# Latent attention: query and key blocks as one paired product for the operand's two parts, emptied by two engines

## What is computed

```python
def _mla_mixer(x, cos, sin, w_in, q_norm, w_qb, kv_norm, w_kvb, w_out):
    proj = x @ w_in
    c_q, c_kv, k_rope, z = jnp.split(proj, [512, 1024, 1088], axis=-1)
    q = (_rmsnorm(c_q, q_norm) @ w_qb).reshape(b, s, 16, 192)
    q_nope, q_rope = q[..., :128], q[..., 128:]
    kv = (_rmsnorm(c_kv, kv_norm) @ w_kvb).reshape(b, s, 16, 128 + 128)
    k_nope, v = kv[..., :128], kv[..., 128:]
    q_rope, k_rope = _rope(q_rope, cos, sin), _rope(k_rope, cos, sin)
    attn = _chunk_causal_attention([q_nope, q_rope], [k_nope, k_rope], v)
    return (attn * jax.nn.silu(z)) @ w_out
```

## Time and profile before

| | us |
|---|---|
| median of 3 runs | 1971.5 (1971.48 to 1973.13) |
| the profiled execution | 1971.0 |
| its span, first to last instruction | 1969.5 |
| granted TensorE clock in the span | 1.00 (2.4 GHz) |

### The profile page before, as it was taken

How to read it: one execution, slowest core, us unless ns; L and a number is a source line. 1 busy time by engine, 2 the same in 40 slices (tenths; PEclk the granted TensorE clock), 3 DMA queues, 4 the chain that set the end, 5 groups by cost and what they waited for, 6 DMA issues and landing times.

```text
span 1969.5 us, 28727 instructions
## 1 busy us (share of the span) xinstructions
PE 1963.2 (100%) x11370; PEld 1716.8 (87%) x11370; DVE 1368.8 (69%) x2117; ACT 1049.3 (53%) x1640; POOL 0.2 (0%) x4
## 2 busy tenths in 40 slices
PE   9999999999999999999999999999999999999999
PEld 7889988988888888898888888888888888888888
DVE  6756778986567676898778887666665556666554
ACT  5645555765456754575566655544443344444432
POOL 0000000000000000000000000000000000000000
PEclk9999999999999999999999999999999999999999
DMA  8554325455543455545533345555555555555562
GB/s 323 184 184 168 129 107 193 171 198 193 192 143 136 180 186 190 192 172 195 214 129 145 118 163 193 192 191 193 192 186 181 192 190 192 193 185 186 190 213 103
DMA packets 52874, 353.43 MB, mean 179 GB/s; under 512 B 5781, under 2 KB 9373, under 8 KB 11013
## 3 DMA queue, kind: packets, MB, share of 16 engines
q1 hardware_dynamic: 50016, 348.84, 48.9%
q10 hardware_dynamic: 2724, 2.75, 0.4%
HBM read 349.47 MB, written 2.11 MB: 179 GB/s over the span
## 4 chain that ended last, share of the span: by engine, by line
PE 94%; DVE 4%; ACT 1%; issue 0%; DMA 0%; ACTq 0%; DVEq 0%
PE bank L1117 94%; DVE WL L2052 2%; DVE AR L2229 0%; ACT WH L1542 0%; DVE AR L2342 0%; DVE XP L2225 0%; DVE AR L2339 0%; DVE XP L2327 0%; PE bank L1256 0%; DMA X<-in_x 0%; DVE AR L2218 0%; DVE AR L2253 0%; DVE AR L2252 0%; ACT XP L1673 0%; ACT L1555 0%
## 5 line engine op out<-in xcount | busy, mean ns | idle before, releaser
L2052 DVE TENSOR_TENSOR WL<-raw,WH 128x1024 fp32r<-128x1024 f32 x649 | 787.7, 1222 | 311.7 <-ACT WH L1542 304.2
L1542 ACT ACTIVATE WH<-raw 128x1024 fp32r<-128x1024 f32 x649 | 681.9, 1056 | 452.6 <-PE bank L1117 421.0
L1117 PE MATMUL bank<-XP,WH 128*128 128x512 f32 (+2 forms) x2096 | 668.4, 393 | 1.0 <-DVE WL L2048 0.6
L1117 PEld LDWEIGHTS bank<-XP,WL 128*128 128x128 f32 x2016 | 378.8, 188 | 80.4 <-issue 0.7
L1117 PE MATMUL bank<-FP,WH 128*128 128x512 f32 x1408 | 443.3, 396 | 0.0
L1117 PE MATMUL bank<-XP,WL 128*128 128x256 f32 (+1 forms) x2016 | 409.8, 279 | 0.1
L1117 PEld LDWEIGHTS bank<-XP,WH 128*128 128x128 f32 (+1 forms) x2096 | 329.1, 188 | 8.0 <-DVE XP L2095 1.4
L1117 PEld LDWEIGHTS bank<-FP,WL 128*128 128x128 f32 x1408 | 265.0, 188 | 61.6
L1117 PE MATMUL bank<-FP,WL 128*128 128x256 f32 x1408 | 277.5, 278 | 0.0
L1117 PE MATMUL bank<-AP,WH 128*128 128x512 f32 x704 | 222.1, 396 | 0.0
L1117 PEld LDWEIGHTS bank<-FP,WH 128*128 128x128 f32 x1408 | 215.2, 189 | 0.4
(11 more groups left out here) (325 smaller groups left out, 1708.8 us busy)
## 6 DMA issues: line engine op xcount, KB each, us to landing
raw<-in_W SPq DMA_DIRECT2D x326, 1024.0 KB, 4.8
out<-AR ACTq DMA_DIRECT2D x16, 128.0 KB, 2.4
raw<-in_W SPq DMA_DIRECT2D x3, 512.0 KB, 6.6
X<-in_x SPq DMA_DIRECT2D x3, 512.0 KB, 12.5
AR<-rv SPq DMA_DIRECT2D x1, 1024.0 KB, 5.9
cst<-in_cst SPq DMA_DIRECT2D x1, 899.5 KB, 12.1
raw<-in_W SPq DMA_DIRECT2D x2, 256.0 KB, 4.1
AR<-in_sgu SPq DMA_DIRECT2D x1, 512.0 KB, 5.7
```

The costliest lines, as they stand in the source:

```text
L1117: return pe.matmul(o, lhsT, rhs, start=start, stop=stop)
L1542: ac.activation(w_slot(WH, s), raw_half(hf), ACT.Copy).then_inc(s_hi, 1)
L2052: tt(w_slot(WL, s), raw_half(pl.half_of[s]), w_slot(WH, s).bitcast(F32), ALU.subtract).then_inc(s_lo, 1)
```

## The change

The three kinds of stage become paired, with VectorE as the last to empty them. Each of their 160 tiles issues two products in place of three, each of the 40 blocks fills a whole bank, and each is emptied in two steps: ScalarE copies the second half to the destination, VectorE adds the first half to it. `head_part` names the destination for both engines. The banks, their turns, and the order of the list of steps are the same.

```diff
@@ -400,9 +400,9 @@
 
 STAGES = {}
 for _s in [Stage("c", 9, 16, "dve", 7, 0, (0, 1, 2, 3, 4, 5, 6)), Stage("z", 16, 16, "dve"),
-           *(Stage(f"qr{g}", 2, 4, "act", pair=False) for g in range(4)),
-           *(Stage(f"qn{g}", 4, 4, "act", pair=False) for g in range(4)),
-           *(Stage(f"kn{g}", 4, 4, "dve", pair=False) for g in range(4)), *(Stage(f"v{g}", 1, 4, "act", 0, 512) for g in range(4)),
+           *(Stage(f"qr{g}", 2, 4, "dve") for g in range(4)),
+           *(Stage(f"qn{g}", 4, 4, "dve") for g in range(4)),
+           *(Stage(f"kn{g}", 4, 4, "dve") for g in range(4)), *(Stage(f"v{g}", 1, 4, "act", 0, 512) for g in range(4)),
            Stage("wo0", 16, 16, "dve", 3, 0, (0, 1, 2), half=False, norm=0), Stage("conv", 16, 16, "dve", (AHEAD, 4), 0, (0, 1, 2, 4, 3, 5, 6, 7), ahead=AHEAD),
            Stage("gates", 1, 16, "dve", pair=False),
            Stage("vm", 4, 16, "act", 0, 512), Stage("o", 16, 16, "dve"), Stage("mz", 16, 16, "dve"),
@@ -880,6 +880,10 @@
         mx = [small[:, 8 * i:8 * i + 2] for i in range(2)]
         ss = [small[:, 16 + 8 * i:16 + 8 * i + 2] for i in range(2)]
         sc = float(192 ** -0.5)
+
+        def head_part(kind, g, n):
+
+            return qr[g % 2][n] if kind == "qr" else blk(QKN, 2 * (4 * g + n) + (kind == "kn"))
 
 
         LN_D = [ar(0, 4096), ar(8192, 4096)]
@@ -1613,13 +1617,10 @@
                 h = n
                 if what == "hi":
                     hi(n)
-                elif what[:2] in ("qr", "qn") and what[3:] == " out":
-                    name, g = what[:3], int(what[2])
-                    ac.wait_ge(*done(name, n))
-                    if what[:2] == "qr" and g >= 2:
-                        ac.wait_ge(s_rope, g - 1)
-                    to = qr[g % 2][n] if what[:2] == "qr" else blk(QKN, 2 * (4 * g + n))
-                    ac.activation(to, bank[pl.bank_of[name, n, 0]][:, 0:T], ACT.Copy).then_inc(s_out["act"], 1)
+                elif what[:2] in ("qr", "qn", "kn") and what[3:] == " out":
+                    if what[:2] == "qr" and int(what[2]) >= 2:
+                        ac.wait_ge(s_rope, int(what[2]) - 1)
+                    second_half(what[:3], n, head_part(what[:2], int(what[2]), n))
                 elif what[0] == "v" and what[2:] == " out":
                     g = int(what[1])
                     ac.wait_ge(*done(what[:2], 0))
@@ -2176,10 +2177,8 @@
                         ins = tt(B[q1, :], x1[q2, :], rt[0][q2, :], ALU.subtract)
                     ins.then_inc(s_rope, 1)
                     dv.wait_ge(s_rope, n + 1)
-                elif what[:2] == "kn" and what[3:] == " out":
-                    name, g = what[:3], int(what[2])
-                    dv.wait_ge(*done(name, n))
-                    dv.tensor_copy(blk(QKN, 2 * (4 * g + n) + 1), psum(name, n)).then_inc(s_out["dve"], 1)
+                elif what[:2] in ("qr", "qn", "kn") and what[3:] == " out":
+                    whole(what[:3], n, head_part(what[:2], int(what[2]), n))
                 elif what == "max":
                     S, m = bank[3 + h % 2], mx[h % 2]
                     dv.wait_ge(s_msc, h + 1)
```

## The result

| | before | after |
|---|---|---|
| median of 12 runs, us | 1971.97 (1971.15 to 1973.13) | 1976.45 (1976.16 to 1976.84) |
| ratio | | 1.0022, 95% interval 1.0014 to 1.0030 |
| profiled execution, us | 1971.0 | 1976.5 |
| span, us | 1969.5 | 1975.0 |
| granted TensorE clock | 1.00 | 1.00 |

The account below looks back on a forecast made before the run. TensorE's uninterrupted products were taken to bound the kernel. Waits and restarts of 6.8 us less 1.9 us gave +4.9 us: 1975.9 us profiled, 1976.4 us median; range 1972.6 to 1979.2.

Parts of the forecast that it names:

- gain of the products: In the 160 newly paired tiles, one product less saves 0.012 us each, 1.9 us in all on TensorE's path.
- waits of group 0, to kn0_0: In group 0, TensorE has 5.57 us of work while VectorE's chain takes 8.04 us, so it waits 2.5 us.
- group 1, to kn1_0: In group 1, same VectorE chain, but TensorE has a scores step more to do: a wait of 1.0 us.
- group 2, to kn2_0: In group 2, VectorE's 9.42 us against TensorE's 8.72 us, plus a later ScalarE copy: a wait of 0.9 us.
- group 3, to pv of head 3: In group 3, VectorE's 13.07 us up to gate 2 against TensorE's 10.93 us: waits of 2.0 us.
- restarts: Behind each of the four waits, TensorE's first group of products takes 0.11 us longer, 0.4 us in all.
- The signs that I had named: Expected in the profile: 11210 products, VectorE busy near 1379 us, ScalarE near 1055, paired tiles 0.348 us, waits at named blocks.
- The wait behind the rotation: Between qr block 1 and qn block 1, VectorE's rotation delays the freeing addition: 8.04 us until kn0_0 may start.
- rival in which these small waits vanish: Waits in groups 1 and 2 may vanish, leaving groups 0 and 3: +2.8 us, 1974.3 us; chance 28%.
- the late additions never hold TensorE: Rival: VectorE's additions cause TensorE no wait, so only the 1.9 us gain remains: 1969.6 us; chance 8%.
- rival in which the key blocks wait too: kn block 2 is late by 0.5 us in each group, 2 us more: 1978.4, up to 1980 us; chance 10%.
- rival of a falling clock: Waits halve TensorE's clock for a v block, 5.5 us each: 1982 us for one, 1998 for all four; chance 4%.

Follow-up runs that it names:

- e9: Changed kernel with the rotation moved behind v (group 3: behind max of head 9) and unused banks for group 0's query and key blocks: 1969.89 us against 1972.01 before.
- e1: Changed kernel's paired products, but each block emptied in one step as before, so the result is incomplete: 1969.41 us against 1971.65 for before.
- e3: Changed kernel with each group's rotation moved on VectorE's list behind the last key block's emptying: 1971.90 us against 1971.65 for before.
- e8: Changed kernel with qn0_1, qn0_2 and qn0_3 of group 0 in unused banks 3, 4 and 5, VectorE's list unchanged: 1974.79 us against 1972.01 for before.
- e10: The kernel before, unchanged, run again for a second profile and the scatter of its runs: 1971.47 us (1970.64 to 1972.38).

## Why the prediction was right, step by step

The best measure of each term is e9, which does the same products and has no wait in this stretch.

| term | forecast | measured | from |
|---|---|---|---|
| gain of the products | 1.9 | 1.66 | 101.73 - 100.07 |
| waits of group 0, to kn0_0 | 2.5 | 2.63 | 10.99 - 8.36 |
| group 1, to kn1_0 | 1.0 | 1.05 | 10.93 - 9.88 from its first query block |
| group 2, to kn2_0 | 0.9 | 0.84 | 12.60 - 11.76 |
| group 3, to pv of head 3 | 2.0 | 1.85 | 16.77 - 14.92 from its first query block |
| v of group 3 | 0 | 0.47 | 7.86 - 7.28 from that pv, less its restart |
| restarts | 0.4 | 0.41 | 0.08, 0.11, 0.11 from kn0_0, kn1_0, kn2_0 to v; 0.11 behind pv |
| sum | +4.9 | +5.6 | 107.33 - 101.73 |

**What bounds the kernel** was right: TensorE's stream had no idle time there, and every delay reached the end. The signs that I had named came (11210 products, VectorE busy for 1377.0 us, ScalarE for 1053.9, paired tiles at 0.348 us), and none of those that would have shown it wrong.

**The products**: right in sign and nearly in size; e1 has 1.4 us by the same point, with a short wait of 0.14 us before v of group 0 for its key blocks' copies and a restart behind it, and e9 1.66. Counted from the first product or the v before to the next v, the gain is 0.45, 0.53, 0.35 and 0.32 us in groups 0 to 3, where the 40 tiles of a group were to give 0.48, so the 0.2 us to my 1.9 are missing in groups 2 and 3; why, I haven't followed. By the formula of the Trainium skill ("TensorE: Matmul & The Clock Gate", "Back-to-back issue gap") they would have been worth 0.4, but I had applied it wrongly: the section gives it for a product by itself, and says that in a stream of weight loads and products both set the spacing, with about 131 ns for 512 columns. This stream, which has a weight load for each product, takes 0.23 us for 512 columns (148.54 to 148.77 us in the trace after), so neither figure fits and the rows of before were the better guide.

**The wait behind the rotation** is the step that decided, and it held link by link. The chain was to take 8.04 us from the end of qr0_1. That block ends at 151.33 in the profile after (ScalarE's copy starts at 151.53, 0.20 behind it), and kn0_0 starts at 159.53, 8.20 later. Of the 0.16 us more, 0.12 lie between the addition of qn0_0 and the rest of the rotation (155.67 to 156.13, where I had 0.34), and 0.06 in the hand-over to TensorE (0.10 for 0.04). VectorE idles for 0.90 us before the second addition, as foreseen. In groups 1 and 2 the difference of two long sums came out within 0.1 us. The rival in which these small waits vanish fell. So did the first, that the late additions never hold TensorE; e3 and e8 show that this would have needed another order or other banks.

**Group 3** is the term that was mis-sized. The three waits that I had named are there, 1.85 us for 2.0, but a fourth is not in the sum: v waits for kn3_2, 0.47 us. I had said that the key blocks have little margin and no wait. ScalarE's and VectorE's timelines after:

```profile
245.88 0.42 DVE L2204 TENSOR_TENSOR AR<-bank,AR 128x256 f32<-128x256 f32 x1
...
248.00 0.76 DVE L2070 TENSOR_TENSOR QKN<-bank,QKN 128x256 f32<-128x256 f32 x2 [0.79 <-ACT QKN L1551]
```

```profile
246.33 0.42 ACT L1653 ACTIVATE XP<-AR 128x256 fp32r<-128x256 f32 x1 [2.60 <-DVE AR L2204]
246.65 1.04 ACT L1546 ACTIVATE WH<-raw 128x1024 fp32r<-128x1024 f32 x1
247.60 0.64 ACT L1551 ACTIVATE QKN<-bank 128x256 f32<-128x256 f32 x2
```

kn3_2 has been ready since about 244.6, but ScalarE waits 2.60 us for gate 3 from VectorE, then does a weight half, then copies; VectorE waits 0.79 us for that copy, and v starts at 248.52. VectorE's lateness goes over to ScalarE and comes back. My walk along the two lists took ScalarE to be free here. It is a small case of the rival in which the key blocks wait too. In groups 0 to 2 they don't wait: what their stretches are longer by is the restart behind kn0_0, kn1_0 and kn2_0.

**The hit on the median is better than the working.** 1976.4 against 1976.45 is the sum of two errors of opposite sign. The stretch lost 5.6 us and not 4.9: 0.24 less from the products and 0.47 more at v of group 3. That the median came out right to 0.1 us is luck. And I had carried the 0.5 us by which before's median lay over its profiled execution to the changed kernel. By 12 runs before's median is 1.0 over its profile, and the changed kernel's runs lie within 0.7 us of each other with the median at its profile. Before's runs scatter over 2 to 3 us on each chip, and why isn't settled (e10).

**The clock** was granted at 1.00 through all the waits, 0.2 to 1.7 us of idle time each, so the rival of a falling clock fell, and the failure that the Trainium skill tells of under "A second HAM failure mode: psum-queue depth-cycling" isn't seen here: eight waits in 100 us while the products cycle through three banks.

## What to carry to other kernels

When a bank gets a second engine in its emptying, ask where the releasing instruction stands on that engine's list and not how busy the engine is: a sum of the durations between the block's end and the release, against what TensorE has to do until it wants the bank, gave each wait to 0.15 us here where the lists run straight. Then the cheap repair is to move what stands in front (4 us of rotation behind v, which is free in groups 0 to 2 and costs 0.6 us in group 3) or to give the block another bank; the same instructions in another order were worth 5.9 us, three times what the change could gain. A place that is free for one queue is full for another, so look at all that is behind the moved step, the next weights first; and where two engines hand work to each other, walk both lists, since lateness goes across and comes back.

## What the runs showed of the hardware

A paired tile takes 0.348 us and three products of 256 columns 0.360, with the same 768 columns: one product with its weight load less is worth 0.010 to 0.012 us. An addition that reads a bank which ScalarE has just read starts 0.04 us behind that copy, as in stage z of before. TensorE's granted clock was 1.00 (2.4 GHz) in the stretches with the waits, whose idle times are up to 1.7 us. None of it was against what I had expected, but for the scatter of before's runs: 1.7 to 2.9 us from lowest to highest in the groups of ten and more runs, where no kernel with paired products has more than 1.0.
